# Residual sums in an SBUF ring instead of an accumulating DMA, fewer weight conversions, and forget gates behind the last projections

## The reference, cut to what matters

```python
x = x + 0.5 * swiglu(rmsnorm(x, ffn1_norm), w1, w3, w2)      # DFF = 5632
h = rmsnorm(x, mix_norm); proj = h @ w_in                    # q, k, v of 8 + 4 heads, memory q of 4, 8 forget gates
logf = log_sigmoid(ff + b_forget); c = cumsum(logf)          # (8 heads, 2048)
# 8 forgetting heads: softmax(q k / sqrt(d) + c_t - c_s), causal; 4 block-sparse heads; 4 heads into 256 memory tokens
x = x + concat(heads) @ w_out
x = x + 0.5 * swiglu(rmsnorm(x, ffn2_norm), w1b, w3b, w2b)
```

## Time and profile before

| | |
|---|---|
| time, median of 3 runs | 5105.06 us (5102.74 to 5105.48) |
| profiled execution, its own time | 5099.32 us |
| its span, slowest core (core 6) | 5097.8 us (all cores 5079.0 to 5097.8) |
| PE busy | 4620.7 us, 91% |
| DVE, ACT, POOL busy | 3052.7, 1553.8, 408.2 us |
| moved by the core's 16 DMA engines | 650.49 MB, mean 128 GB/s |

### The profile page before, as it was taken

One profiled execution on the slowest core, in us unless ns is written; L12 is line 12 of the kernel. 1 busy time (PEld: TensorE's weight loads), 2 busy tenths in 40 slices (PEclk: granted clock), 3 DMA queues, 4 the chain that ended last, 5 costly groups with the idle time before them and its releaser, 6 DMA issues.

```text
span 5097.8 us, 64605 instructions; the slowest of 8 cores (5079.0 to 5097.8 us)
## 1 busy us (share of the span) xinstructions
PE 4620.7 (91%) x20297; PEld 1974.4 (39%) x20708; DVE 3052.7 (60%) x5155; ACT 1553.8 (30%) x2697; POOL 408.2 (8%) x589
## 2 busy tenths in 40 slices
PE   5999988869999978889969999889989899999998
PEld 1443433324444433344423223334434344444444
DVE  5656555646565766755534456566555577656574
ACT  2212222112231223556556565212221121212121
POOL 0010000000000000000002221000100000000100
PEclk9999999989999999999989799999999999999999
DMA  8889697875848466423511014996996968484846
GB/s 180 126 174 141 150 160 126 205 134 104 170 95 155 90 206 159 106 59 80 111 64 48 26 51 108 195 173 110 173 167 136 138 127 166 85 151 88 151 85 132
DMA packets 122960, 650.49 MB, mean 128 GB/s; under 512 B 14784, under 2 KB 35712, under 8 KB 66688
## 3 DMA queue, kind: packets, MB, share of 16 engines
q0 software_dynamic: 62352, 473.99, 53.5%
q1 hardware_dynamic: 60272, 172.35, 11.1%
HBM read 788.71 MB, written 201.50 MB: 194 GB/s over the span
## 4 chain that ended last, share of the span: by engine, by line
PE 69%; DMA 14%; DVE 7%; ACT 4%; issue 4%; another core or an unknown queue 1%; DVEq 0%; SPq 0%; ACTq 0%; POOLq 0%; POOL 0%
PE ps L371 68%; DMA wraw_46<-wu 5%; DMA wraw_45<-wu 5%; DVE wcmb_47 L346 1%; DVE wcmb_48 L346 1%; DMA wraw_45<-wo 1%; DMA xst_59<-out 1%; DVE acd_142 L346 1%; DMA xst_59<-xr 1%; DMA wraw_46<-wdb_2 1%; ACT hrb_89 L368 1%; ACT hrb_88 L368 1%; DVE XA L346 1%; DVE XA L350 1%
## 5 line engine op out<-in xcount | busy, mean ns | idle before, releaser
L371 PE MATMUL ps<-XA,wcmb_47 128*128 128x512 bf16 x3998 | 932.4, 388 | 52.3 <-DVE t_c_53 L346 44.7
L371 PE MATMUL ps<-XA,wcmb_48 128*128 128x512 bf16 x4000 | 913.4, 382 | 47.5 <-DVE t_c_53 L346 33.2
L346 DVE TENSOR_TENSOR wcmb_47<-wraw_45 128x1024 bf16<-128x1024 bf16 (+1 forms) x790 | 504.9, 671 | 387.8 <-DMA wraw_45<-wu 312.9
L346 DVE TENSOR_TENSOR wcmb_48<-wraw_46 128x1024 bf16<-128x1024 bf16 (+1 forms) x790 | 505.0, 671 | 288.9 <-DMA wraw_46<-wu 182.3
L371 PEld LDWEIGHTS ps<-XA,wcmb_47 128*128 128x128 bf16 x4080 | 400.6, 99 | 553.2 <-issue 102.1
L371 PEld LDWEIGHTS ps<-XA,wcmb_48 128*128 128x128 bf16 x4080 | 397.4, 98 | 533.0 <-issue 71.9
L371 PE MATMUL ps<-XB,wcmb_48 128*128 128x512 bf16 x2271 | 518.8, 382 | 85.6 <-DVE yst_58 L346 80.5
L371 PE MATMUL ps<-XB,wcmb_47 128*128 128x512 bf16 x2271 | 517.1, 381 | 19.2 <-ACT t_e_50 L363 9.0
L371 PE MATMUL ps<-XA,wraw_45 128*128 128x512 bf16 x1594 | 387.5, 390 | 25.7 <-DVE XA L346 23.7
L363 ACT COPY t_e_49<-ps 128x512 f32<-128x512 f32 x328 | 191.3, 583 | 719.7 <-PE ps L371 623.7
L371 PE MATMUL ps<-XA,wraw_46 128*128 128x512 bf16 x1597 | 378.3, 383 | 2.2 <-issue 0.4
(11 more groups left out here) (395 smaller groups left out, 4799.6 us busy)
## 6 DMA issues: line engine op xcount, KB each, us to landing
wraw_45<-wu POOLq DMA_DIRECT2D x88, 1024.0 KB, 14.5
wraw_46<-wu POOLq DMA_DIRECT2D x88, 1024.0 KB, 10.6
out<-yst_57 POOLq DMA_DIRECT2D x48, 1024.0 KB, 8.9
out<-yst_58 POOLq DMA_DIRECT2D x48, 1024.0 KB, 9.0
xst_59<-out SPq DMA_DIRECT2D x24, 1024.0 KB, 10.1
xst_60<-out SPq DMA_DIRECT2D x24, 1024.0 KB, 11.6
wdb_2<-wd_2 POOLq DMA_DIRECT2D x16, 1024.0 KB, 29.4
wraw_45<-wdb_2 POOLq DMA_DIRECT2D x16, 1024.0 KB, 6.5
```

Of the source, the lines that this page charges most:

```text
L346: return op(eng, lambda e: e.tensor_tensor(out=o_, in0=a, in1=b, op=alu), R=[a, b], W=[o_])
L371: return op("pe", lambda e: e.matmul(o_, l, r, start=start, stop=stop, skip_group_check=skip), R=[l, r], W=[o_])
```

## The change

1. **Ring.** In down 0 and down 1 of all four ffn calls, `dquads_sum` replaces the accumulating DMA: the old residual (x itself in down 0 of the first layer half, else `out`) is loaded by SP, three dquads ahead, into a ring of four tiles (`yst` and `xst`), DVE adds the four outputs (four more instructions of 128 x 512 in each dquad), and SP stores. The first half of the output projection uses the ring of four too. `dquads_acc`, the accumulating form, stays in down 2 without statistics and in the second half of the output projection.
2. **No copies.** `xcopies` goes.
3. **Weights.** `conv` stays for block 2 alone, and goes through SBUF: POOL loads and casts into `cvb`, SP stores. Down 0 and down 1 load their f32 weights with a cast, twice.
4. **Schedule.** `membg` moves from up 1 to up 0 of ffn(0, 0); the statistics move to up 1 of ffn(0, 0) and to up 0 of ffn(0, 1) and ffn(1, 0).
5. **Start.** Two of the four gain products of each x tile move to POOL ahead of the statistics, and two of the four scalings become POOL products; `w_prep(0)` moves ahead; the first weight loads wait for one x tile more.
6. **Forget gates.** They become background steps of the last 8 projection quads, with cumulative sums, transposes and the loads of the first attention head.

```diff
+        cvb = [sb("cvb%d" % i, [128, 4096], BF16, (164 + 8 * i) * KB) for i in range(2)]
+        def conv(f):
+            def g(i):
+                dma("pool", cvb[i % 2][:, :], wd[f][2][i], "cvl%d" % (i % 2), R=[])
+                dma("sp", wdb[f][i], cvb[i % 2][:, :], "cvs%d" % (i % 2), W=[("wd", f, i)])
+            return [lambda i=i: g(i) for i in range(8)]
...
+                        ft[f, tp, b, dp] = add(wdb[f][dp], nb, [("wd", f, dp)]) if b == 2 else add(wd[f][b][dp], nb)
...
-            w_load(0, R=[xs0[3][:, 0, 0:1]])
-            w_load(1, R=[xs0[6][:, 0, 0:1]])
+            w_load(0, R=[xs0[4][:, 0, 0:1]])
+            w_load(1, R=[xs0[7][:, 0, 0:1]])
...
+                for i, k in ((1, c), (2, 8 + c)):
+                    ts(xs0[c][:, i, :], xs0[c][:, i, :], gT[:, k:k + 1], ALU.mult, "pool")
...
-                stt(X[:, 5, c, :], xs0[c][:, 1, :], g0[c], rb[1][:, :], ALU.mult, ALU.mult)
+                tt(X[:, 5, c, :], xs0[c][:, 1, :], rb[1][:, :], ALU.mult, "pool")
...
-                stt(X[:, 6, c, :], xs0[c][:, 2, :], g1[c], rb[0][:, :], ALU.mult, ALU.mult)
+                tt(X[:, 6, c, :], xs0[c][:, 2, :], rb[0][:, :], ALU.mult, "pool")
...
-                dquads([ft[f, tp, b, dp] for dp in range(8)], XB, tp, stats and b == 2)
+                tl = [ft[f, tp, b, dp] for dp in range(8)]
+                if b < 2:
+                    dquads_sum(tl, XB, tp, xr if f == 0 and b == 0 else out, yst + xst, False)
+                elif stats:
+                    dquads_sum(tl, XB, tp, out, yst, True)
+                else:
+                    dquads_acc(tl, XB, tp)
...
+        def dquads_sum(tl, X, tp, src, ring, stats):
+            n = len(ring)
             def yload(dp, i):
+                dma("sp", ring[dp % n][:, i, :], src[tp, dp, :, i * 512:(i + 1) * 512], "yl%d%d" % (dp % n, i), R=[rt(tp, dp)[i]])
+            for dp in range(n - 1):
+                for i in (1, 2, 3, 0):
+                    yload(dp, i)
             for dp in range(8):
+                y = ring[dp % n]
                 def acc(i, dp=dp, y=y):
                     def g(v):
                         tt(y[:, i, :], y[:, i, :], v, ALU.add)
+                        if stats:
...
+                        dma("sp", out[tp, dp, :, i * 512:(i + 1) * 512], y[:, i, :], "ys%d%d" % (dp % n, i), W=[rt(tp, dp)[i]])
+                        if dp + n - 1 < 8:
+                            yload(dp + n - 1, i)
                     return g
                 quad(tl[dp], X, tmp["s12"][:, :], tmp["s11"][:, :], acc(1), acc(2), acc(3), acc(0))
...
+            bg.extend(forget())
             for t, p in zip(pt_a1, A1_P):
                 pquad(t, p, 1, True)
...
+            return [prep, gate(0), gate(1), gate(2), gate(3), sum1, sum2, first_loads]
...
-        ffn(0, 0, sched((0, 1, xcopies(0)), (5, 1, conv(0, 0)), (14, 1, membg()), (15, 1, conv(0, 1)), (29, 1, conv(0, 2)), (28, 2, xstats(xr, "X", 1))),
-            xbuild(XA, xr, "X", 1, 0), False)
-        ffn(0, 1, sched((0, 1, xcopies(1)), (14, 1, xstats(out, "R", 0))), xbuild(XA, out, "R", 0, 1), True)
+        ffn(0, 0, sched((0, 1, membg()), (14, 1, xstats(xr, "X", 1)), (29, 1, conv(0))), xbuild(XA, xr, "X", 1, 0), False)
+        ffn(0, 1, sched((1, 1, xstats(out, "R", 0))), xbuild(XA, out, "R", 0, 1), True)
         projection()
-        forget()
         attention()
         outproj()
-        ffn(1, 0, sched((0, 1, conv(1, 0)), (15, 1, conv(1, 1)), (14, 1, xstats(out, "R", 1)), (29, 1, conv(1, 2))), xbuild(XA, out, "R", 1, 2), False)
+        ffn(1, 0, sched((1, 1, xstats(out, "R", 1)), (29, 1, conv(1))), xbuild(XA, out, "R", 1, 2), False)
         ffn(1, 1, [], [], False)
```

More of the change, by code:

```diff
@@ L867, in projection @@
             drain()
-        SPT = sb("SPT", [8, S], F32, 188 * KB)
         def forget():
[L872 to L880, removed]
+            wf32 = sb("wf32", [128, 128], F32, 178 * KB)
@@ new lines, in go @@
+                def go():
+                    p = ps[6][0:8, :]
+                    for a, (wi, xi) in enumerate(terms):
+                        for k in range(8):
+                            mm(p, wfs[:, wi, k * 8:(k + 1) * 8], X[:, xi, k, :], a == 0 and k == 0, a == 1 and k == 7)
+                    actf(eb[:, :], p, AF.Exp, bias=negb[0:8, :], scale=-1.0)
+                    actf(SPT[:, i * 512:(i + 1) * 512], eb[:, :], AF.Ln, bias=sml[0:8, 1:2])
+                return lambda: defer(2, go)
@@ L914, in cprep, with sum1 @@
+            def sum1():
                 vset(onesr[:, :], 1.0)
@@ new lines, in build, with kind_of, ring, loads @@
+        MR = [sb("am%d" % i, [8, 1024], BF16, (16 + 2 * i) * KB) for i in range(2)]
+        def kind_of(h):
+            return "fox" if h < 8 else ("moba" if h < 12 else "mem")
+        cnt = {"q": 0, "k": 0, "c": 0, "m": 0}
+        def ring(n, r):
+            i = cnt[n] % 2
+            cnt[n] += 1
+            return i, r[i]
+        def loads(h):
+            kind, d = kind_of(h), {}
+            i, d["q"] = ring("q", QR)
+            dma("sp", d["q"][:, :], QTs[h], "aq%d" % i, R=[("Q", h)])
+            if kind != "mem":
+                i, d["k"] = ring("k", KR)
+                d["v"] = VR[i]
+                dma("sp", d["k"][:, :], KTs[h], "ak%d" % i, R=[("K", h)])
+                dma("sp", flat(d["v"]), Vs[h], "av%d" % i, R=[("V", h)])
+            if kind == "fox":
+                i, d["c"] = ring("c", CR)
+                dma("sp", d["c"][:, :], cs3[:, h, :], "ac%d" % i, R=[("cs", 0), ("cs", 1), ("cs", 2)])
+            if kind == "moba":
+                i, d["m"] = ring("m", MR)
+                dma("sp", d["m"][:, :], MRs[h - 8], "am%d" % i, R=[("MR", h - 8)])
+            return d
@@ L958, in attention, with first_loads @@
+        first = {}
+        def first_loads():
+            first[12] = loads(12)
+        def attention():
             tc = [0]
@@ L1082, in attention @@
             horder = [12, 13, 14, 15, 8, 9, 10, 11, 0, 1, 2, 3, 4, 5, 6, 7]
-            nxt = loads(horder[0])
+            nxt = first.pop(12)
             for hi_, h in enumerate(horder):
```

153 lines of the change are left out of this document (54 added, 99 removed).

## The result

The changed kernel takes 4954.7 us (median; 4941.9 to 4961.2) beside 5103.9 us for the kernel before: a ratio of 0.971, interval 0.969 to 0.973. The forecast was 4966 us. The profiled execution falls from a span of 5097.8 us to 4959.7 us, by 138.1 us; the steps' sum had been 139.4.

The account below looks back on a forecast made before the run. DMA engines were taken to set the time outside the plain stages, which PE fills. Savings of -187.4 us plus 48 for the ring gave -139.4, so 4966 us (forecast case 4945 to 4990; whole range 4915 to 5050).

Parts of the forecast that it names:

- steps 1 and 3: Copies gone from down 2 of ffn(0, 0), 55.7 us gained; block 2's conversion through SBUF, up 2 there 24.9 gained.
- Step 1: Down 2 of ffn(0, 0), without the x copies, becomes its twin in ffn(1, 0): 157.3 to 101.6 us, 55.7 gained.
- Step 2: Six up stages: conversions of blocks 0 and 1 go, statistics and the memory's work move; sum -74.8 us.
- a rival (0.06): Up stages beside the ring: its stocked loads and last stores delay their weights, giving back 50 us, 5016; chance 0.06.
- Step 4: Start of the kernel: products split between DVE and POOL end earlier, a late weight-load wait goes; -15 us (-16 to +2).
- I take 34: Start: the last x tile, arriving at 39.6 us with copies beside it, was taken to arrive at 34 without them.
- 16 x 0.65: Start: POOL's 16 gain products at 0.65 us each, from 34.6 to 45 us.
- both bounds: Start: all 32 POOL instructions at 1.41 us give +2.5; all at 0.61, with DVE's own instructions holding the end, -12.
- Step 5: Forget gates moved into projection quads: 21.4 and 12.9 us saved, 15 for gate matmuls and 2 charged; -17 (-19 to -6).
- the bank I looked at: Projection quads: PE needs the next DVE result (bank of product 2) seven products later, so sums are covered; 2 us charged.
- Step 6: Eight down stages with the ring: y loads and stores exceed DMA time by 6.6 us; +6 a stage, +48 (0 to +128).
- my price: Ring in down stages: 3.75 us of all 16 engines per y load or store, +6 us a stage, +48 in all.

## Why the prediction was right, and where it was not

- *What bounds it, steps 1 and 3.* Right: where DMA engines were shared with copies and conversions, taking the transfers away gave the stage of the twin. Step 1 misses some 10 us on the slowest core (111.4 us against 101.6); by the medians of the changed kernel the stage takes 107.6 and its twin 104.0. It keeps a few us, whose cause stays open.
- *Step 2.* Right in five of six stages. Up 1 of ffn(0, 0) missed its 185.0, with 204.3, because the moved statistics load right behind a ring stage, and into a tile of the ring; I had the ring's last stores under a rival (0.06), and the sum put them at nothing. With the statistics three quads later it takes 182.3.
- *Step 4 is the step that failed*, in price and in sign: +19.9 for -15 (-16 to +2). "I take 34" for the last x tile: 39.9. "16 x 0.65" for the gain products: 16 x 1.58, for which I had taken a cast as the nearest row. The x tile comes no sooner without the copies beside it. And both bounds assumed that DVE works beside POOL's products, while DVE was held until the last of them at 85.6 and still had some 18 us of chunks to do.
- *Step 5*, right sign, too small. The gates cost the last seven projection quads 33 us (92 to 126), not 17: 64 products as charged (14.4 us busy), but the sums did stop PE, for 5.00 and 3.95 us. The first stop is a head's transposition that stands behind DVE's result, earlier than the bank I looked at; the second is the 16 transposes themselves. Of the remaining 10 us a part may be the clock, 0.95 over these quads against 1.00 before. So what the step spends, 33 us, is about what it takes away, 21.4 + 12.9, and nearly all of its gain is the granted clock of the attention, which the sum did not contain. The right sign is luck. The place of the transposes accounts for 22 us in the changed kernel and 33 in the kernel before. Why the clock falls late and only on some cores with the transposes ahead of the fifth head stays open.
- *Step 6*, the mechanism was right, the size was not. With the measured 3.4 us a transfer instead of 3.75 the same balance is 6 x 5.15 + 2 x 5.9 + 13 x 3.4 = 86.9 against 84.8, +2.1 a stage; measured +1.4 (1.7 by medians) and about 20 us in up 1. It is a small difference of large terms: a tenth off the price takes two thirds of it, and the 3.4 us may hold lost slack too, so the fit proves little. (At 2.6 a transfer the balance is 76.5, not 76.8; nothing hangs on it.) The stages fill their engines so nearly that one transfer more made the kernel slower than before (5178 against 5107). The Trainium skill's figure (HBM Reference, "Specifications (TRN2)") gave 11.0 us a dquad, +26 in all; over whole stages 703.4 / 64 = 11.0 was measured (10.8 before, +14), so here it came nearer than my price. It does not show that figure as the limit: PE was busy 84.88 of the 87.7 us of the first ring stage shown.

## What to carry to other kernels

Before work goes to POOL, look for the time of an instruction of the same operation and type, not of any on that engine, and ask which DVE instructions run beside it: where one holds up the other, as the two-input products did here, they finish one behind the other. A DMA stage near its limit is judged by its slack in time (how early a transfer is asked for) and by what the next stage's loads stand behind, not by its share alone. And a short run of narrow products in front of a stage can cost more by the clock that follows than by its own time; here moving it was one line. A forecast that is met in sum says little until its terms are read one by one.

## What the runs showed of the hardware

- A DMA share of 0.98 stood beside a ring stage in which PE was busy 84.60 of 85.8 us, and 0.99 beside one of 102.4 us that waited for its transfers: the share alone did not tell them apart.
- One DVE sum of 0.42 us took 18.41 us beside fifteen back-to-back two-input POOL products, and 0.43 where the next product waited for it. Beside POOL's gain products DVE was not held so: five weight sums took 3.59 us instead of 3.09.
- Sixteen transposes of 8 x 128 values, 1.1 us of PE, were followed by some 60 us at half the granted clock on all eight cores when the heads with three-row products came next. When projection quads came next, no core was at half for more than 7 us at a time behind them; in the first forget head, later, two of eight cores were at 0.83 over 60 us.
